# A decoder step in split float32r: the weights' low part by an accumulating DMA, high-part products first

## What is computed

```python
xn = rmsnorm(x, norm_mix)
proj = xn @ w_in                         # 1024 x 9216, split in nine parts
ya = (a_b * causal_dwconv3(a_c * a_x)) @ w_out_a
yb = silu(layernorm(causal_dwconv31(b_val * sigmoid(b_glu)) + bias)) @ w_out_b
yx = softmax(q @ mem_k.T / 16) @ mem_v @ w_out_x
g = sigmoid(gate_logits + b_gate)
h = x + (g[0] * ya + g[1] * yb + g[2] * yx) @ w_o
hn = rmsnorm(h, norm_ffn)
h = h + (silu(hn @ w_ff_gate) * (hn @ w_ff_up)) @ w_ff_down
y = rmsnorm(h, norm_final)               # mem_k, mem_v and conv states are outputs too
```

## Times and profile before

| | |
|---|---|
| median of 3 runs | 1226.22 us (1224.56 to 1231.22) |
| span of the profiled execution | 1226.2 us |
| TensorE, matmuls | 1158.7 us busy, 9320 matmuls |
| VectorE | 641.7 us busy |
| GpSimd | 479.1 us busy |
| ScalarE | 342.2 us busy |
| DMA | 127.71 MB, mean 104 GB/s |

### The profile page before, as it was taken

How to read it: one execution, slowest core, us unless ns; L and a number is a source line. 1 busy time by engine, 2 the same in 40 slices (tenths; PEclk the granted TensorE clock), 3 DMA queues, 4 the chain that set the end, 5 groups by cost and what they waited for, 6 DMA issues and landing times.

```text
span 1226.2 us, 22162 instructions
## 1 busy us (share of the span) xinstructions
PE 1158.7 (95%) x9320; PEld 1147.0 (94%) x9320; DVE 641.7 (52%) x854; ACT 342.2 (28%) x468; POOL 479.1 (39%) x198
## 2 busy tenths in 40 slices
PE   4899999999799979999999999999999999999995
PEld 3899998898799979999999999999999999999994
DVE  6545998865687586879611474224433433410013
ACT  3442222241011032222222462333222223211132
POOL 4664442121133153353543434334444444444440
PEclk9999999998689799999999999999999999999998
DMA  8574232344344122323323223422332332332211
GB/s 255 162 230 148 69 103 75 115 161 138 103 138 139 35 69 70 103 71 102 105 69 103 97 76 100 142 70 73 99 103 69 102 102 70 102 113 95 82 40 70
DMA packets 118303, 127.71 MB, mean 104 GB/s; under 512 B 2260, under 2 KB 115924, under 8 KB 118223
## 3 DMA queue, kind: packets, MB, share of 16 engines
q1 hardware_dynamic: 98006, 102.89, 26.0%
q10 hardware_dynamic: 20233, 23.87, 5.9%
HBM read 122.34 MB, written 5.41 MB: 104 GB/s over the span
## 4 chain that ended last, share of the span: by engine, by line
PE 49%; issue 35%; POOL 13%; DVE 2%; ACT 1%; POOLq 0%; DVEq 0%; ACTq 0%
PE acc L1408 47%; POOL w_l L448 12%; PE acc L1656 1%; DVE ubyb L1258 1%; DVE ubyb L1244 0%; ACT junk L821 0%; DVE y_st L1358 0%; DVE sg L1240 0%; PE acc L1375 0%; DVE big_l L1249 0%; PE acc L1658 0%; ACT w_h L463 0%; POOLq L442 0%; PE acc L1620 0%; POOLq L446 0%
## 5 line engine op out<-in xcount | busy, mean ns | idle before, releaser
L448 POOL TENSOR_TENSOR w_l<-w_raw,w_h 128x1024 fp32r<-128x1024 f32 x188 | 478.1, 2564 | 715.7 <-ACT w_h L463 715.7
L1408 PE MATMUL acc<-big_h,w_h 128*128 128x260 f32 x2016 | 421.6, 291 | 24.0 <-DVE sg L1147 10.2
L1408 PE MATMUL acc<-big_h,w_l 128*128 128x260 f32 x2016 | 413.1, 287 | 0.0
L1408 PE MATMUL acc<-big_l,w_h 128*128 128x260 f32 x2016 | 412.5, 287 | 0.0
L1408 PEld LDWEIGHTS acc<-big_h,w_h 128*128 128x128 f32 x2016 | 318.0, 193 | 25.8 <-DVE sg L1147 10.6
L1408 PEld LDWEIGHTS acc<-big_h,w_l 128*128 128x128 f32 x2016 | 317.9, 193 | 0.0
L1408 PEld LDWEIGHTS acc<-big_l,w_h 128*128 128x128 f32 x2016 | 317.6, 193 | 0.0
L986 DVE SCALAR_TENSOR_TENSOR ubyb<-ubyb,prm 128x512 f32<-128x512 f32 (+1 forms) x240 | 265.5, 1106 | 22.7 <-DVE ubyb L986 18.1
L463 ACT ACTIVATE w_h<-w_raw 128x1024 fp32r<-128x1024 f32 x188 | 188.1, 1049 | 224.3 <-PE acc L1408 192.7
L1408 PE MATMUL acc<-hg_h,w_h 128*128 128x260 f32 x704 | 141.9, 283 | 0.0
L1408 PE MATMUL acc<-hg_h,w_l 128*128 128x260 f32 x704 | 141.9, 283 | 0.0
(11 more groups left out here) (190 smaller groups left out, 854.5 us busy)
## 6 DMA issues: line engine op xcount, KB each, us to landing
w_raw<-in_w_in_dram SPq DMA_DIRECT2D x36, 1024.0 KB, 5.0
w_raw<-in_w_ff_gate_dram SPq DMA_DIRECT2D x11, 1024.0 KB, 5.3
w_raw<-in_w_ff_up_dram SPq DMA_DIRECT2D x11, 1024.0 KB, 5.3
k_st<-in_cache_mem_k_dram ACTq DMA_DIRECT2D x8, 1024.0 KB, 5.1
v_st<-in_cache_mem_v_dram ACTq DMA_DIRECT2D x8, 1024.0 KB, 5.0
w_raw<-in_w_ff_down_dram SPq DMA_DIRECT2D x8, 1024.0 KB, 5.0
w_raw<-in_w_k_dram SPq DMA_DIRECT2D x4, 1024.0 KB, 11.8
w_raw<-in_w_v_dram SPq DMA_DIRECT2D x4, 1024.0 KB, 6.1
```

Of the source, the lines that this page charges most:

```text
L448: nc.gpsimd.tensor_tensor(w_l[:, j, ks, :], w_raw[:, j, ks, :], f(w_h[:, j, ks, :]), ALU.subtract).then_inc(w_lo, 1)
L1408: last = M.matmul(out[:, b, 0:HALF], w, xs[:, k_at + k, b * HALF:(b + 1) * HALF], start=start and k == 0 and w is wh and xs is x[0], stop= ...
```

## The change

The low part is made another way. After its two high halves ScalarE runs one copy more, over the whole chunk, with scale -1: the output is float32r, so `w_l` then holds minus the high part. That copy counts the new semaphore `w_neg` up. GpSimd no longer computes. For each of the 94 chunks it waits for `w_neg` and issues a DMA that reads the same 1 MB of weights from memory a second time and adds it into `w_l` (`accum_op=ALU.add`), which leaves `w - w_h` there; its landing counts `w_rest0` or `w_rest1` (one for each slot). GpSimd's loop is written out, since each issue names its own weights.

SyncE's loads into `w_raw` now wait for `w_neg` in place of `w_lo`. On TensorE each `tile` is parted in `tile_hi` (two products, 32 matmuls, waiting for `w_hi`) and `tile_lo` (one product, 16 matmuls, waiting for `w_rest`). A `chunk` runs both tiles' high parts and then both low parts; keys and values, `w_o` and the down projection are reordered likewise. The queries and the C and X tiles of branch A run high and low part tile by tile. The number of matmuls and their shapes stay.

```diff
@@ SyncE
-                    sp.wait_ge(w_lo, c * 2 - 2)
+                    sp.wait_ge(w_neg, c[0] * c[1] + (c[2] - 1))
...
@@ GpSimd
-            with pool.Fori(0, C_END // 2) as i:
...
-                        nc.gpsimd.tensor_tensor(w_l[:, j, ks, :], w_raw[:, j, ks, :], f(w_h[:, j, ks, :]),
-                                                ALU.subtract).then_inc(w_lo, 1)
+            def add_raw(c, src, col, k0=0, kn=KT):
+                pool.wait_ge(w_neg, c + 1)
+                pool.dma_start(w_l[:, c % 2, 0:kn, :], src[:, k0:k0 + kn, col:col + CW],
+                               accum_op=ALU.add).then_inc(w_rest[c % 2], 16)
+            for c in range(8):
+                add_raw(C_KV + c, wk if c < 4 else wv, (c % 4) * CW)
...
@@ ScalarE, hi_part
                     nc.scalar.activation(w_h[:, slot, ks, :], w_raw[:, slot, ks, :], ACT.Copy).then_inc(w_hi, 1)
+                nc.scalar.activation(w_l[:, slot, :, :], w_raw[:, slot, :, :], ACT.Copy, scale=-1.0).then_inc(w_neg, 1)
@@ TensorE
+            def tile_hi(slot, j, use, x, k_at=0, ks=KT, start=True, first_half=None, ready=None,
+                        beside=None):
...
+                        pe.wait_ge(w_hi, first_half(k // HK))
+                    for xs in x:
                         for b in range(2):
+                            last = M.matmul(out[:, b, 0:HALF], w_h[:, slot, k, cols],
+                                            xs[:, k_at + k, b * HALF:(b + 1) * HALF],
+                                            start=start and k == 0 and xs is x[0], stop=False)
...
+            def tile_lo(slot, j, use, x, k_at=0, ks=KT, stop=True, loaded=None):
...
+                    pe.wait_ge(w_rest[slot], turn(loaded) * 16)
+                for k in range(ks):
+                    for b in range(2):
+                        last = M.matmul(out[:, b, 0:HALF], w_l[:, slot, k, cols],
+                                        x[0][:, k_at + k, b * HALF:(b + 1) * HALF],
+                                        start=False, stop=stop and k == ks - 1)
...
@@ TensorE, chunk
                 for j in range(2):
                     free(use + j)
-                    tile(slot, j, static + j, x, ready=None if j else ready,
-                         first_half=None if j else (lambda s: c * 2 + (s + 1))).then_inc(acc_done, 1)
+                    tile_hi(slot, j, static + j, x, ready=None if j else ready,
+                            first_half=None if j else halves_of)
+                for j in range(2):
+                    tile_lo(slot, j, static + j, x, loaded=None if j else c).then_inc(acc_done, 1)
```

More of the change, by code:

```diff
@@ L1387, in flip8_back @@
                 last.then_inc(acc_done, 1)
[L1389 to L1394, removed]
+            def tile_hi(slot, j, use, x, k_at=0, ks=KT, start=True, first_half=None, ready=None,
+                        beside=None):
                 out = acc[use % 4]
+                cols = slice(j * P, (j + 1) * P)
                 for k in range(ks):
@@ L1436, in _ @@
                         pe.wait_ge(nrm_lo, m + 1)
+                    rows = slice(m * P, (m + 1) * P)
                     for k in range(KT):
                         if m == 0 and k % HK == 0:
[L1439 to L1443, removed]
+                            pe.wait_ge(w_hi, 2 * c + k // HK + 1)
+                        for n in range(2):
+                            M.matmul(acc[use % 4][:, m, 0:CW], mn[n][:, k, rows], w_h[:, c % 2, k, :],
+                                     start=k == 0 and n == 0, stop=False)
+                pe.wait_ge(w_rest[c % 2], turn(c) * 16)
+                for m in range(2):
+                    rows = slice(m * P, (m + 1) * P)
+                    for k in range(KT):
+                        last = M.matmul(acc[use % 4][:, m, 0:CW], mn[0][:, k, rows], w_l[:, c % 2, k, :],
+                                        start=False, stop=k == KT - 1)
                 last.then_inc(acc_done, 1)
@@ L1597, in beside @@
                                 last.then_inc(acc_done, 1)
[L1598 removed]
+                    tile(half, 0, u0, xn, c=C_CX + q, beside=beside).then_inc(acc_done, 1)
                 else:
[L1600 removed]
+                    tile(half, 0, u0, xn, c=C_CX + q).then_inc(acc_done, 1)
                 free(u0 + 2)
@@ L1643, in _ @@
                     free(use)
-                    tile(c % 2, j, use, br, stop=False, ready=None if c + j else (m_lo, 0),
-                         first_half=None if j else (lambda s: 2 * (C_WO + c) + s + 1))
+                    tile_hi(c % 2, j, use, br, ready=None if c + j else (m_lo, 0),
+                            first_half=None if j else halves_of)
+                for j in range(2):
+                    tile_lo(c % 2, j, T["wo"] + 2 * c + j, br, stop=False, loaded=None if j else C_WO + c)
                 if c == 0:
@@ L1690, in _ @@
                             free(use)
-                        last = tile(c % 2, j, use, mid, k0, kn, start=g == 0, stop=g == 2,
-                                    first_half=None if j else (lambda s: 2 * c + s + 1))
+                        tile_hi(c % 2, j, use, mid, k0, kn, start=g == 0, first_half=None if j else halves_of)
+                    for j in range(2):
+                        last = tile_lo(c % 2, j, T[f"d{p}"] + j, mid, k0, kn, stop=g == 2,
+                                       loaded=None if j else c)
                         if g == 2:
```

77 lines of the change are left out of this document (53 added, 24 removed).

## The result

The changed kernel takes 1235.78 us (median of 20 runs, 1231.88 to 1242.03) beside 1226.34 us for the kernel before on the same chip (20 runs). The ratio is 1.009, 95% interval 1.0071 to 1.0109. It is slower, as forecast, but by 9.4 us and not by the 25 us of the forecast.

A forecast was written before the change was run, and what follows sets the result against it. TensorE's matmuls bound the kernel, with waits on VectorE and a slowed clock in the earlier half. Sum: 1226 - 40 + 10 + 5 + 8 + 30 + 12 = 1251 us; range 1200 to 1400.

The forecast's parts named there:

- Term 1: Mainly 85 to 600 us: without GpSimd's subtraction, TensorE's waits on VectorE and slow clock shrink, -40 us (ends 0, 52).
- Term 2: Each chunk's accumulating DMA: issue 2.6, engine time 6.7, load beside 3.3, fixed 2.0, landing 14.6 us (ends 5.3, 20.1).
- Term 3: Landings past the hidden 13.7 us in the feed-forward cost +10 us there, +5 elsewhere, +8 with the caches.
- the ring: Feed-forward: beyond 13.7 us, two slots set the pace; landing 14.6 gives 11.98 us a chunk, 0.45 more, 10 for 22.
- The +8 for the caches: Chunks C and X, where `k_st` and `v_st` load too: landing 3.3 us longer, 1 us for each of 8 chunks.
- the +5 for scatter: Other stages and down projection, where ScalarE starts at once and the threshold is about 15 us: 5 us for scatter.
- Term 4: Keys and values, first 85 us: ten accumulating DMAs need 38 us too much, some 8 give way, +30 (+5 to +63).
- Term 5: Six seams and layernorm: first tiles end 3.8 us later, ScalarE's copy precedes sigmoids; 2 us each, +12 (0 to 25).
- (a): Accumulating DMA costs little more than a plain load, decided from about 4.5 us engine time: 1203 us, chance 0.27.
- (b): Gain and loss nearly cancel, DMA engine time between 4.5 and 5.5 us: 1223 us, within 0.5%, chance 0.10.
- (c): DMA engines become the bound from 8.2 us engine time a chunk; with 10.0, 1416 us; chance 0.23.
- (d): VectorE is disturbed as before: 1291 us; counted on the forecast's side, chance 0.40 for both together.

The follow-up runs named there:

- Order_only: Changed kernel's TensorE order, but low parts by GpSimd's subtraction for all 94 chunks, no accumulating DMA, no extra ScalarE copy: 1224.99 us, ratio 1.0009 to the kernel before.
- plain_copy: Changed kernel with GpSimd's 94 DMAs overwriting `w_l` instead of adding into it: 1208.64 us, ratio 0.989 to the kernel before.
- Tile_by_tile: Changed kernel with each tile's high part then low part run in turn, instead of both high parts first: 1284.81 us, ratio 1.052 to the kernel before.
- keys_subtract: Changed kernel with GpSimd's subtraction kept for the first 8 chunks (keys and values), other 86 by accumulating DMA: 1200.23 us, ratio 0.983 to the kernel before.
- extra_traffic: Changed kernel with SyncE copying one further megabyte, memory to memory, for each of 22 feed-forward chunks: 1246.18 us, one run.
- short_minus: Changed kernel with ScalarE's scale -1 copy cut to one of 8 row groups from chunk 2 on: 1223.45 us, ratio 0.998 to the kernel before.

## Why the prediction was right in direction, and where it failed

**Term 1, the subtraction goes, -40 us: right.** Chunks 12 to 36 win 40.7 us. The stretch between these two chunks, before and after:

```profile
118.50:520.10 401.60, 372.36 (x2824) 364.78 (x2823) 309.50 (x455) 92.51 (x139) 124.26 (x48) 0.92 0.31 100
155.90:516.90 361.00, 353.68 (x2825) 346.98 (x2825) 231.05 (x452) 135.38 (x163) 37.27 (x24) 0.97 0.80 182
```

By its two parts: the 18.2 us of waits went fully, and the low clock cost 0.08 x 401.6 = 32 us before and 0.03 x 361 = 11 us after, an estimate of 21 us won. Together that is 39. The low clock that is left has another cause than VectorE's conv steps. TensorE's work around 310 us (first row 310 to 320, second 320 to 330), beside the earlier trace rows:

```profile
310.00:320.00 10.00, 4.72 (x22) 3.62 (x21) 8.68 (x29) 1.58 (x3) 0.00 (x0) 0.87 1.13 258
320.00:330.00 10.00, 10.00 (x50) 10.00 (x48) 0.79 (x2) 0.00 (x0) 0.00 (x0) 0.50 0.04 14
```

After a stretch 4.72 of 10 us busy the granted clock is 0.50 here too, the lower level, with the conv steps undisturbed; TensorE waits 2.5 us there for VectorE's `p` of the sample rows' attention. So this fall, which the prediction laid to the slow conv steps, comes without them as well. Order_only shows that nothing in the order is behind the gain; the vanished waits and the steady conv steps show that the missing subtraction is. The Trainium skill, "SBUF — State Buffer", section "Who interferes with whom", has a second half that no row of before could show, that a GpSimd instruction which only writes does not contend; no run here shows it, since none has such an instruction beside the conv steps. What the trace of after has there are GpSimd's DMA issues of 1.55 us, and beside them no conv step is over 755 ns.

**Term 2, the landing, 14.6 us: too large, 11.2 measured.** Its engine time was right, 6.63 for 6.7. The issue is 1.55 us, not the middle of 0.37 and 4.8. The load beside costs 2.6, not 3.3: the last megabyte, issued at 1187.50 us when no load is left, lands in 8.6. (The end of the accumulating DMA before it, which lands at 1189.81, is still beside its start.) And 8.6 is only 0.4 more than 1.55 + 6.63; the very last DMA, 768 KB and quite alone, took 7.37, 1.0 more than its issue of 1.44 and 4.97 of packets. So half or more of the 2.0 us "fixed" of a plain load was counted twice. Three middles or sums, each on the slow side, gave 3.4 us.

That "two reads" is the reason for the engine time is not shown. The prediction took SyncE's 3.33 us twice. Beside the loads plain_copy shows 5.2 us for one read by the same queue, so 1.9 us come with the queue that GpSimd feeds and 1.4 with the adding. With nothing else moving it divides otherwise. The last DMA of plain_copy (first row) and of after (second row), 48 packets on each engine:

```profile
1173.20:1178.10 4.90, 4.90 (x43) 4.90 (x43) 0.00 (x0) 4.75 (x11) 0.82 (x1) 1.00 0.62 161
1201.30:1208.80 7.50, 7.50 (x65) 7.50 (x64) 0.00 (x0) 5.67 (x12) 1.44 (x1) 1.00 0.71 105
```

That is 0.62 x 4.90 / 48 = 0.063 us a packet plain and 0.71 x 7.50 / 48 = 0.111 with adding: for 64 packets 0.7 us more than SyncE's for the queue, and 3.1 for the adding. A plain packet of this queue takes longer beside other transfers, an accumulating one does not, and why stays open. The Trainium skill, "Collectives: The Full Stack", section on the bandwidth ceiling, gives a ratio of 1.93 for two source reads; the runs show 1.99 against SyncE's queue, 1.27 against a plain copy by the same queue beside the loads and 1.75 alone, and here the measurement decides.

**Term 3, is it in time?, +23 us: this step failed.** The term took the 14.6 us of Term 2 as past the threshold of 13.7; the landing was 11.2, and the 23 us did not come. The threshold was right as far as the runs show. With 11.2 us the ring gives (9.35 + 11.2) / 2 = 10.3 us, under the 11.53 of the matmuls, with 2.5 us to spare; 14.6 stood 0.9 over. In the timeline of the feed-forward loop ScalarE, SyncE and GpSimd do what the prediction laid out:

```profile
905.07 2.00 ACT L495 ACTIVATE w_h<-w_raw 128x1024 fp32r<-128x1024 f32 x2
906.97 1.90 ACT L496 ACTIVATE w_l<-w_raw 128x2048 fp32r<-128x2048 f32 x1
908.90 0.37 SPq L373 DMA_DIRECT2D w_raw<-in_w_ff_up_dram  x1
909.29 1.55 POOL L454 DMA_DIRECT2D w_l<-in_w_ff_up_dram  x1 [10.17 <-ACT w_l L496]
```

The issue comes 4.2 us after the start of the high part (the prediction: 4.1), the landing 10.6 later, at 919.8; the low products are wanted at 905.07 - 1.4 + 11.53 + 7.69 = 922.9. Nothing waits, and chunks 66 to 81 lose nothing. The 2.3 us of the loop are lost at its start, where order_only loses 1.7 too. The +8 for the caches did not come either (chunks 20 to 27 gain 12.3 us, by the same timeline), nor the +5 for scatter. Without this term the prediction's own sum is 1226 - 40 + 30 + 12 = 1228 us, the case within 0.5%; with the measured sizes it is 1226 - 40.7 + 37.5 + 10.7 = 1233.5, the span of the profiled execution, as it must be, since the three are read from one table. Tile_by_tile is the check from the other side: where the cover is really short, the formula gives the time of a chunk behind chunk 66 to 0.13 us (12.25 for 12.37).

**Term 4, the first stage, +30 us: right in kind, 37.5 in size (35.6 by keys_subtract).** DMA share in the first 120 us:

```profile
0.00:120.00 120.00, 73.01 (x491) 70.32 (x492) 39.86 (x63) 51.91 (x57) 15.16 (x19) 0.87 0.97 233
```

0.97 x 120 = 116 us of engine time, as the 56 + 67 - 8 = 115 of the prediction. But the 8 us of other traffic taken off the time had to be moved before chunk 12 all the same: the plain 38 was the answer. Since extra_traffic shows packet times adding to more than the span, that the sum comes out at the span here is not proof of its form; that the DMAs set the pace of this stage is. Plain_copy takes 14.0 us off it by cheaper packets and a shorter issue, and short_minus, with 1.5 us less of ScalarE's copy in each chunk, only 2. Whether it is what the engines can carry or the length of each landing, the runs do not separate.

**Term 5, seams, +12 us: 10.7, right in size by luck.** The prediction laid it to first tiles that end later. Order_only has these late tiles and loses 2.1 us from chunk 36 on, and plain_copy, which has them and ScalarE's copy, 0.9. What costs here is `w_l` that comes late, and with a landing of 8.1 us instead of 11.2 nearly all of it goes. More than half of it is one seam, 6.4 us at the start of the output of branch A. There ScalarE's high part is held as before the change (5.10 us by VectorE's `uao`, L1225), but now its copy and the DMA come behind:

```profile
582.41 2.01 ACT L495 ACTIVATE w_h<-w_raw 128x1024 fp32r<-128x1024 f32 x2 [5.10 <-DVE uao L1225]
584.33 1.90 ACT L496 ACTIVATE w_l<-w_raw 128x2048 fp32r<-128x2048 f32 x1
...
586.52 1.55 POOL L454 DMA_DIRECT2D w_l<-in_w_out_a_dram  x1 [15.15 <-ACT w_l L496]
```

TensorE then waits 4.9 us, the row among the waits above. Without most of ScalarE's copy (short_minus) 5.6 of the 10.7 us go too. The copy, the issue and the landing follow one another, so shortening any of them counts, and the shares do not add up. The prediction had named the copy only as something that could make it wrong, by the tiles that it delays.

**The rivals.** (a) was refuted in its condition: the DMA costs 6.63 us of engine time, over the 4.5 from which it decides. But its other half, that D is below 12 and term 3 goes, held: a short landing and dear engine time went together, which the prediction had tied apart. (b), within 0.5%, missed by a little. (c) did not come, and its threshold of 8.2 us was not a threshold: extra_traffic put a plain megabyte more on each chunk and lost 0.5 us, not 1.8. (d) is refuted by the steady 752 ns.

## What to carry to other kernels

A transfer under a pipeline of matmuls costs nothing until its landing passes the cover, and then it costs in every turn. So work out the cover, and compare it with a landing whose overlapping parts are not added up. Look for the stage with the least arithmetic per byte first, since an edit that doubles the traffic everywhere costs most there (37.5 us of 48 here), and it can be left out there: subtraction for 8 chunks of 94 turned a loss of 9.4 us into a gain of 26. An order that gives nothing by itself can still be what makes the other half of a change affordable (49 us here).

## What the runs showed of the hardware

- A packet of 1 KB took 0.052 us on SyncE's queue. On the queue fed by GpSimd it took 0.081 us in the mean of plain_copy and 0.063 us with nothing beside it, and with adding 0.104 and 0.111 us. GpSimd's issue took 0.87 us for a plain megabyte and 1.55 us for an accumulating one.
- An accumulating megabyte landed in 8.6 us with no load beside it, in 11.2 us beside one and in 13.9 us beside a load and a copy.
- The DMA share by packet times can pass one (1.07 over 255 us), so a share near one is no proof that nothing more goes through (0.86 went to 1.07 for 0.5 us a chunk).
- Two GpSimd instructions with two SBUF inputs and an SBUF output behind a DMA issue stretched single conv steps from 0.75 to 3.9 us, more than the 2.95 us beside the subtraction of before.
